# A state-space scan whose chunk states are stored adjacently, with carries in doubling steps, corrections tile by tile, and gating between its steps

## What is computed

```python
x_re = jnp.einsum('bngc,gpc->bngp', ug, bb_re)      # 64 groups, 16 channels, 64 states
x_im = jnp.einsum('bngc,gpc->bngp', ug, bb_im)
...
_, _, s_re, s_im = lax.associative_scan(combine, (l_re, l_im, x_re, x_im), axis=1)
y = (jnp.einsum('bngp,gcp->bngc', s_re, c_re)
     - jnp.einsum('bngp,gcp->bngc', s_im, c_im)).reshape(b_, n, D_MODEL)
y = jax.nn.gelu(y + d * uf)
out = (y @ w_glu_v) * jax.nn.sigmoid(y @ w_glu_g)
```

## Time and profile before

| | us |
|---|---|
| median of three runs | 2287.75 |
| the three runs | 2287.75, 2288.28, 2266.84 |
| the profiled execution: its time | 2266.89 |
| its span | 2264.6 |
| mean granted TensorE clock | 0.969 of full |
| PE busy | 2127.8 (94%) |
| DVE busy | 1087.0 (48%) |
| ACT busy | 745.5 (33%) |
| POOL busy | 157.2 (7%) |

### The profile page before, as it was taken

The page is one execution under the profiler, slowest core; times in us unless marked ns, Lnnn a source line. Parts: engine busy times, 40 slices in busy tenths (PEclk is TensorE's granted clock), DMA queues, the critical chain, the costliest instruction groups (busy, mean ns, idle before and its releaser), DMA issues.

```text
span 2264.6 us, 46747 instructions
## 1 busy us (share of the span) xinstructions
PE 2127.8 (94%) x19825; PEld 2020.4 (89%) x19825; DVE 1087.0 (48%) x1563; ACT 745.5 (33%) x1080; POOL 157.2 (7%) x250
## 2 busy tenths in 40 slices
PE   7999999974899999999999999988888799999998
PEld 6999999953899999999999999975656599999998
DVE  5453676697344445322654442234763234544422
ACT  4222222543343343222422222242543124434211
POOL 3002010140000000000000000000027100000000
PEclk9999999997999999999999999999999799999999
DMA  6232323100222333332333333221237322333332
GB/s 134 84 107 71 93 85 107 39 3 6 85 84 85 93 93 88 103 90 63 95 92 93 93 101 90 79 80 29 50 105 203 88 66 78 90 93 93 105 90 77
DMA packets 355924, 192.56 MB, mean 85 GB/s; under 512 B 33005, under 2 KB 350443, under 8 KB 355795
## 3 DMA queue, kind: packets, MB, share of 16 engines
q1 hardware_dynamic: 348736, 180.19, 27.8%
q0 software_dynamic: 5488, 9.03, 1.4%
q10 hardware_dynamic: 1570, 1.48, 0.3%
HBM read 184.23 MB, written 3.02 MB: 83 GB/s over the span
## 4 chain that ended last, share of the span: by engine, by line
PE 85%; DVE 7%; ACT 3%; SPq 2%; issue 2%; DMA 1%; DVEq 0%; ACTq 0%
PE ps L1724 75%; PE ps L1737 2%; DVE stmp L466 2%; PE ps L2132 1%; PE ps L2257 1%; DVE xs L470 1%; PE ps L2288 1%; SPq L440 1%; SPq L438 1%; DVE stmp L469 1%; PE ps L2019 1%; PE ps L1743 1%; DVE wl L1126 1%; PE ps L2235 1%; DMA xin<-x_prompt 0%
## 5 line engine op out<-in xcount | busy, mean ns | idle before, releaser
L1724 PE MATMUL ps<-xh,wh 128*128 128x260 f32 x3296 | 870.1, 285 | 30.8 <-DVE xl L1441 15.8
L1724 PE MATMUL ps<-xl,wh 128*128 128x260 f32 x3296 | 863.6, 284 | 0.0
L1724 PE MATMUL ps<-xh,wl 128*128 128x260 f32 x3296 | 667.4, 284 | 0.0
L1724 PEld LDWEIGHTS ps<-xh,wh 128*128 128x128 f32 x3296 | 626.9, 190 | 37.7 <-issue 30.6
L1724 PEld LDWEIGHTS ps<-xl,wh 128*128 128x128 f32 x3296 | 625.0, 190 | 0.0
L1724 PEld LDWEIGHTS ps<-xh,wl 128*128 128x128 f32 x3296 | 512.1, 190 | 0.0
L650 ACT ACTIVATE wh<-raw 128x1024 fp32r<-128x1024 f32 (+1 forms) x150 | 175.6, 1170 | 597.7 <-PE ps L1724 596.5
L1126 DVE TENSOR_TENSOR wl<-raw,wh 128x1024 fp32r<-128x1024 f32 (+1 forms) x150 | 206.1, 1374 | 238.9 <-ACT wh L650 238.8
L1724 PE MATMUL ps<-hh,wh 128*128 128x260 f32 x1056 | 277.7, 284 | 0.0
L1724 PE MATMUL ps<-hl,wh 128*128 128x260 f32 x1056 | 275.6, 282 | 0.0
L668 ACT ACTIVATE wh<-raw 128x1024 fp32r<-128x1024 f32 (+1 forms) x124 | 135.3, 1091 | 418.3 <-PE ps L1724 418.3
(11 more groups left out here) (403 smaller groups left out, 2200.3 us busy)
## 6 DMA issues: line engine op xcount, KB each, us to landing
raw<-ffn_w_gate SPq DMA_DIRECT2D x88, 512.0 KB, 3.8
raw<-ffn_w_up SPq DMA_DIRECT2D x88, 512.0 KB, 3.8
raw<-ffn_w_down SPq DMA_DIRECT2D x64, 704.0 KB, 4.5
cb<-cache_ckv SPq DMA_DIRECT2D x72, 128.0 KB, 2.8
cb<-cache_ckv POOLq DMA_DIRECT2D x56, 128.0 KB, 2.9
raw<-s_w_glu_v SPq DMA_DIRECT2D x8, 512.0 KB, 3.8
raw<-s_w_glu_g SPq DMA_DIRECT2D x8, 512.0 KB, 3.7
raw<-mla_w_o SPq DMA_DIRECT2D x8, 512.0 KB, 4.1
```

The lines of the kernel that those rows point to most:

```text
L1724: got = mm(ps[0:width, bank + half, 0:HALF], w[par_][:, k * width:k * width + width], src[:, k0 + k, half * HALF:half * HALF + HALF], star ...
```

## The change

1. `xs` becomes [128, re/im, 32 pairs, 8 (m), 9 (b)]: the blocks b of one m lie side by side, in rows nine apart. ACT's `chunk_inputs` writes it with two instructions for each of re and im. PE's `from_states` reads it with b outside and m inside, nine words apart.
2. The carries take three doubling steps (distance 1, 2, 4) with two more powers `mu2`, made by POOL; the corrections run tile by tile, 4 pairs and 7 x 7 numbers at once, and raise `s_sc` per tile.
3. During scan part 2, DVE runs a piece of the gating of tiles 0 to 3 after each step (`first_tiles`).
4. d u is added to the taps matrix (`s_kd`), so the gating reads PSUM and `ta` is not needed. `ct` copies for tiles 2 to 5 move from POOL to ACT, written out between ACT's other work. Bank 3 serves tiles 3 and 7.
5. `xh` and `xl` stay in position order; the addition to x turns the order back.
6. PE: taps and from_states 2 and 3 in turns, then taps 4 to 7, then from_states 4 to 7; the GLU waits for `s_q7` and for the tiles one by one.

```diff
-                u, xs, s0, sn, wba = take(
-                    a, ("u", [P, KD, TOK], F32), ("xs", [P, 2, NPAIR, NCH + 1], F32), ("s0", [P, 2, NPAIR, NB], F32),
+                u, xs, sn, wba = take(
+                    a, ("u", [P, KD, TOK], F32), ("xs", [P, 2, NPAIR, NBK, NB8 + 1], F32),
...
+            def block(m, b0, b1):
+                return xs[:, :, lo:hi, 0, b0 + 1:b1 + 1] if m == NBK - 1 else xs[:, :, lo:hi, m + 1, b0:b1]
...
             for m in range(1, NBK):
-                own(advance(blk[:, :, :, :, m], blk[:, :, :, :, m - 1], 0, nb))
-            for b in range(1, nb):
-                own(advance(blk[:, :, :, b:b + 1, NBK - 1], blk[:, :, :, b - 1:b, NBK - 1], NBK - 1, 1))
-            for m in range(NBK - 1):
-                got = advance(blk[:, :, :, 1:nb, m], blk[:, :, :, 0:nb - 1, NBK - 1], m, nb - 1)
+                advance(block(m, 0, NB8), block(m - 1, 0, NB8), mu[:, 0], NB8)
+                if beside is not None:
+                    beside(step)
+                step += 1
+            for s, coef in ((1, mu[:, NBK - 1]), (2, mu2[:, 0]), (4, mu2[:, 1])):
+                advance(block(NBK - 1, s, NB8), block(NBK - 1, 0, NB8 - s), coef, NB8 - s)
...
+            for n0 in range(lo, hi, QP):
...
+                        got = tt(both[i][r], mu[:, 0:NBK - 1, 2 * i + r, n0:n0 + QP].rearrange("p m n -> p n m").unsqueeze(3).to_broadcast([P, *size]),
+                                 xs[:, i, n0:n0 + QP, 0, 1:NB8].unsqueeze(2).to_broadcast([P, *size]), ALU.mult)
...
+                own(tt(tmp[:, 0, 0:2 * w], tmp[:, 0, 0:2 * w], tmp[:, 1, 0:2 * w], ALU.add))
+                for r in range(2):
+                    part = xs[:, r, n0:n0 + QP, 1:NBK, 1:NB8]
+                    got = tt(part, part, both[0][r], ALU.add)
+                got.then_inc(done, 1)
...
-                run(xs[:, :, QP * t:QP * t + QP, 1:NCH + 1], x_ps[:, :, :, 0:NCH], ACT.Copy)
+                for r in range(2):
+                    x_b = x_ps[:, r, :, 0:NCH].rearrange("p q (b m) -> p q m b", m=NBK)
+                    run(xs[:, r, QP * t:QP * t + QP, 1:NBK, 0:NB8], x_b[:, :, 0:NBK - 1, :], ACT.Copy)
+                    run(xs[:, r, QP * t:QP * t + QP, 0, 1:NB8 + 1], x_b[:, :, NBK - 1, :], ACT.Copy)
...
+                if t >= 2:
+                    act.wait_ge(xl_rdy, GEN["glu"] + t - 1)
+                run(tb[:, t % 2, 0:SEQ], ps[:, Y_BANK[t], :], ACT.Square, scale=math.sqrt(0.044715)).then_inc(s_y2, 1)
...
+            tt(ktc[:, :, 0, :], ktc[:, :, 0, :], dd, ALU.add).then_inc(s_kd, 1)
...
+            chunk_scan(own, tt, stmp, NPAIR // 2, NPAIR, s_sc, first_tiles)
+            argument(4)
+            for t in range(5, KD):
+                gated(t - 1)
+                argument(t)
+                lo_out(t - 1)
...
-                tt(x[:, d, :], x[:, d, :], tb[:, j, :], ALU.add).then_inc(x_upd, 1)
+                tt(x[:, d, SEQ:TOK], x[:, d, SEQ:TOK], tb[:, j, SEQ:TOK], ALU.add)
+                by_step = x[:, d, 0:SEQ].rearrange("p (c i) -> p i c", i=L)
+                tt(by_step, by_step, tb[:, j, 0:SEQ].rearrange("p (i c) -> p i c", i=L), ALU.add).then_inc(x_upd, 1)
...
-                pe.wait_ge(s_sc, 1 if t < KD // 2 else 2)
+                pe.wait_ge(s_sc, t + 1)
...
-                                             xs[:, r, QP * t + q, 0:NCH], start=False, stop=i == L - 1 and r == 1, skip_group_check=True)
+                                             xs[:, r, QP * t + q, :, 0:NB8].rearrange("p m b -> p b m"), start=False, stop=i == L - 1 and r == 1, skip_group_check=True)
...
-            for t in range(2, KD):
+            pool.wait_ge(s_ct, CT[5])
+            for t in range(6, KD):
                 out_matrices(t)
```

More of the change, by code:

```diff
@@ L469, in advance @@
                 own(tt(both[0], both[0], both[1], ALU.add))
[L470 removed]
+                own(tt(dst, dst, both[0], ALU.add))
+            step = 0
             for m in range(1, NBK):
[L473 to L481 removed]
+                advance(block(m, 0, NB8), block(m - 1, 0, NB8), mu[:, 0], NB8)
+                if beside is not None:
+                    beside(step)
+                step += 1
@@ L881, in _, with out_matrices @@
             tap_blocks(3)
+            def out_matrices(t):
+                act.wait_ge(s_ct, CT_0 if t == 2 else CT[t - 1])
+                act.wait_ge(s_yp, t - 1)
+                for h in range(2):
+                    rows = slice(NS * h, NS * h + NS)
+                    for r in range(2):
+                        last = run(ct[rows, t % 2, :, r, :].rearrange("p j (q h c) -> p j q h c", q=QP, h=2)[:, :, :, h, :],
+                                   ctc[rows, r, QP * t:QP * t + QP, :, :].rearrange("p q j c -> p j q c"), ACT.Copy)
+                last.then_inc(s_ct, 1)
@@ L882, in _ @@
+            squared(0)
+            sigmoid(0)
+            hi_out(0)
+            out_matrices(3)
+            squared(1)
+            sigmoid(1)
+            hi_out(1)
+            tap_blocks(4)
+            squared(2)
+            sigmoid(2)
+            hi_out(2)
+            out_matrices(4)
+            squared(3)
+            sigmoid(3)
+            hi_out(3)
             act.wait_ge(s_fp, 1)
-            run(s0[:, :, :, :].rearrange("p r n b -> p (r n b)"), ps[:, 6, :], ACT.Copy).then_inc(s_fe, 1)
@@ L884, in _ @@
-            tap_blocks(4)
+            run(sn[:, :, :, :].rearrange("p r n b -> p (r n b)"), ps[:, 6, :], ACT.Copy).then_inc(s_fe, 1)
             tap_blocks(5)
+            out_matrices(5)
             tap_blocks(6)
+            tap_blocks(7)
             act.wait_ge(s_fe, 1)
@@ L1400, in _ @@
             dve.wait_ge(s_ctc, L)
-            dve.wait_ge(s_w, W_MU)
[L1402 to L1405, removed]
+            same = stmp[:, 0, 0:GC]
+            own(V.tensor_reduce(same, cst[:, C_ST:C_ST + NS].rearrange("p (k c) -> p c k", c=GC), AX.X, ALU.add))
+            dd = stmp[:, 1, 0:KD * GC].rearrange("p (t c) -> p t c", c=GC)
@@ L1442, in _ @@
+            chunk_scan(own, tt, stmp, NPAIR // 2, NPAIR, s_sc, first_tiles)
+            argument(4)
+            for t in range(5, KD):
+                gated(t - 1)
+                argument(t)
+                lo_out(t - 1)
+            dve.wait_ge(s_q6, 1)
+            tt(xl[:, :, SEQ:TOK], ysb, xh[:, :, SEQ:TOK], ALU.subtract).then_inc(s_q7, 1)
             gated(KD - 1)
@@ L2518, in _ @@
                 m = 2 * m
-                if m < NBK:
+                own(last)
+            for k in range(2):
+                src = mu2[:, 0] if k else mu[:, NBK - 1]
+                t0, t1 = (kfree[:, 256 * i:256 * i + 2 * NPAIR].rearrange("p (r n) -> p r n", r=2) for i in range(2))
+                T(t0, src[:, 0:1, :].to_broadcast([P, 2, NPAIR]), src[:, 0:2, :], ALU.mult)
+                own(T(t1, src[:, 1:2, :].to_broadcast([P, 2, NPAIR]), src[:, 2:4, :], ALU.mult))
+                own(T(mu2[:, k, 0:2, :], t0, t1, ALU.add))
+                G.tensor_scalar(mu2[:, k, 2, :], mu2[:, k, 1, :], -1.0, None, ALU.mult)
+                last = G.tensor_copy(mu2[:, k, 3, :], mu2[:, k, 0, :])
+                if k == 0:
                     own(last)
```

167 lines of the change are left out of this document (97 added, 70 removed).

## The result

The changed kernel takes 2255.87 us in the median of 20 runs (2242.34 to 2274.50), the kernel before 2286.72 in the median of 20 runs beside them (2266.80 to 2291.83). The ratio is 0.9892, with a 95% interval from 0.9869 to 0.9916: about one per cent faster. The forecast was 2266.7, within 2240 to 2279.

What follows compares the result with a forecast made beforehand. It took one chain, DVE alone then DVE and ACT in turns from 450.16 to 572.10 us, as the bound. Its terms put the GLU at 551.0, 21.1 sooner: 2287.75 - 21.1 = 2266.7 us, range 2240 to 2279.

Steps and rivals of the forecast that it cites:

- Chunk inputs: ACT's unpacking before the scan: four instructions for one, 0.5 us more a tile, mostly hidden; scan starts at 450.7.
- Part 1: First scan part on DVE: 27.0 us of own work plus 5 of surcharge beside POOL's copies, 32.0 us.
- Part 2: Second scan part on DVE with gating between steps: 482.7 to 520.7, with 0.7 a tile operation and 1.5 of late ACT answers.
- Adjacency: DVE's scan operations on xs in runs of 8 and 7: 1.1 ns a number, bounds 1.04 and 1.9.
- Taps 5: PE's start of taps 5 after ACT's taps block 5: 520.2, after some 9 us of idleness.
- A tile from states: PE's matmuls reading xs nine words apart: 2.5 us a tile, bounds 2.00 (no effect) and 4.0 (double).
- the ring: ACT and DVE alternating over the last tiles' output, remainder, square, sigmoid and product: 3.4 us a turn.
- Rival 2: PE pays for the stride of xs, 4 us a tile: GLU at 555, 17 gained, 2271; chance 0.12.
- GLU: In the GLU, x's big addition goes from 0.70 to about 1.3 us; priced at nothing, 0.6 with no cover.
- 0.37 + 3 x 0.47: DVE's scan step over 256 numbers in the new layout, summed to 1.75 us against 2.33 before.
- Rival 3: PE pays far more for the stride: slower from 7.8 us a tile, 18 slower at 10, 2306; chance 0.04.
- such a fall of the median: The measured median falling into the lower group of runs, as one of three did; adds about 0.15.

Runs made afterwards that it cites:

- the second profile: The changed kernel itself run once more with nothing altered, profiled at full clock in the chunk inputs: 2244.69 us.
- the run of the scan alone: The kernel before with only the new layout, doubling scan and tile-wise corrections, without interleaved gating or moved copies: 2251.43 us, ratio 0.9881.
- the two runs in turns: The changed kernel with taps and from_states alternating on PE and ACT's work earlier: states read in stored order 2255.45 us, with step 9 2239.28 us.
- the fill: Dense fp32 products that nobody reads, added before the chunk inputs: five on the changed kernel 2250.48 us, five on the kernel before 2281.36 us.

## Why the prediction was right, step by step

At the clock of the profile behind the prediction the sum held almost to the microsecond: the GLU at 550.52 against 551.0, 21.6 us gained against 21.1, 22.2 in time. The mechanism was right: the shorter scan alone gives 19 of the 22. That the sum came so near is in part luck, for two of its errors cancel. Step by step, in the second profile:

- **Chunk inputs.** Scan from 449.82, predicted 450.7. The four copies for one cost nothing that shows.
- **Part 1** 32.25 us, predicted 32.0 (27.0 of work and 5 of surcharge). It was right as a sum: the work is about 26 and POOL takes 6. Single steps go from 1.72 to 3.0 us beside POOL's copies (453.25, 461.40), and the last doubling step takes 3.9 beside POOL's arithmetic for the sample, where the same step takes 1.2 in part 2. In the run of the scan alone, with POOL's copies beside part 2 as well, part 2 took 33.1 us.
- **Part 2** 35.8 us, predicted 38.0. The gating operations cost 0.61 each and not 0.7, and the waits for ACT came to 1.8 us, priced at 1.5.
- **Adjacency.** 256 numbers in runs of eight take 0.42 to 0.43 us, the same as over adjacent scratch, and 0.46 from start to start, so about 1.04 ns a number beside the 0.2 us, the near end of my bounds. Every other row begins at an odd word. The Trainium skill (Vector Engine (DVE) Microarchitecture Reference, Measured stream behaviour on trn2) gives 1.30 ns for pairs that begin so; with runs of eight no such loss is to be seen.
- **Taps 5** at 517.49, predicted 520.2, after 7.34 us of idleness; and 14.0 us for the three, as predicted.
- **A tile from states** is the term that was mis-sized: 2.5 us predicted, 4.0 measured. The steps of 16 bytes and more double the pass. And even without it the term had been 3.9, for the four tiles stand back to back. That could be read before. The first profile of the kernel before has tiles back to back, the second of these 3.9 us behind the first:

```profile
500.28 2.00 PE L2047 MATMUL ps<-xs,ct 128*32 128x64 f32 x127 [0.38 <-issue]
504.18 2.00 PE L2047 MATMUL ps<-xs,ct 128*32 128x64 f32 x128 [1.90 <-issue]
```

I took the 2.00 of a tile between taps and left the 1.90 of "issue" beside it unread. The loss was hidden by the 2.8 us won in front (the last four tiles start at 531.49, not 534.3) and by the ring: I had the last tiles 3.4 us apart through ACT and DVE, and they came 3.8 to 3.9 apart through PE. Rival 2, which had the right price for the tile, put the GLU at 555 for the same reason: it kept the late start of taps 5.
- **GLU.** The big addition to x takes 1.20 us in place of 0.70, ACT's square waits 2.7 us for it instead of 2.1, and PE is busy all of 560 to 580 us. Priced at nothing, rightly.
- **Slips in the working.** 0.37 + 3 x 0.47 is 1.78 and not 1.75, 0.2 us a part; measured 1.72. Rival 3 has the kernel even at 7.8 us a tile and 18 slower at 10: with the four tiles that it names that is 9, and 18 would take all eight.

**The number.** 2266.7 was the median of three runs less 21.1, and the measured one is 10.8 below it. What I had not seen is that the gain depends on the clock. At half clock in the chunk inputs the kernel before loses 12.7 us of the GLU's start and the changed one 21.1 (550.52 to 571.60). The first profile of the changed kernel shows where:

```profile
503.24 0.22 DVE L1504 TENSOR_TENSOR rbc<-rbc,ps 128x64 f32<-128x64 f32 x1 [7.32 <-PE ps L2148]
```

Part 2 of the scan begins at 492.62 there, 10.6 us later than at full clock. After its first step DVE has a piece of the sample's gating to do, and waits 7.32 us for the sample's product on PE, which stands behind the late chunk inputs and taps; the scan ends at 538.20, 20.4 later, and ACT's taps block 5, the taps and the tiles are as late as that. In the kernel before, the sample's gating stands behind the scan and does not wait for PE. So the interleaving ties the scan to PE, and the prediction had no term for it, since its profile had the full clock.

The gain is 22 in one pair of profiles and 13 in the other, yet the median fell by 31, because more runs of the changed kernel (10 of 20) than of the kernel before (3 of 20) fell in their lowest group. The part of the 31 beyond 22 is the mixture and nothing that the prediction worked out; it gave such a fall of the median 0.15. Whether the change raises that chance or the sample was kind stays open: in the twelve later runs the changed kernel had four in its lowest group and a median of 2264.44, and the kernel before had medians of 2281.58, 2277.18 and 2278.16 in its later sets.

## What to carry to other kernels

When a stage is cut short on one engine, look up who paces the next one before counting the rest of the gain: here the scan alone gave 19 of 22 us, and some 16 more lay in PE's and ACT's order and in the stride of PE's operand. An operation that is moved in between the steps of a long chain brings its own waits into the chain: ask what it waits for when the engine that feeds it is late. Price a block of small matmuls by the distance from one to the next where they stand back to back, "issue" included, and keep the moving operands of such small fp32 matmuls at a step of at most two numbers: scatter on the PSUM side instead, which cost nothing here. When the times of a kernel lie in groups, profile until each group has a profile, and compare like with like; a median over groups says more of their mixture than of the change.

## What the runs showed of the hardware that was not expected

- 128 matmuls of 64 fp32 numbers take 2.0 to 2.2 us with steps of 1 and 2 in the moving operand, and 3.6 to 4.2 us with steps of 4, 8, 9 and 16; PSUM written with a step of 8 costs nothing (2.00).
- PE's instructions came in packets of about 16 KB, one for 128 small matmuls with their weight loads. No two packets started less than 3.2 us apart in fourteen traces; tiles of 2.00 us back to back came every 3.9 us, with halts of 1.6 to 1.9 us. That the packets set this pace is likely, not shown.
- The granted clock fell to half at 434 us in six of ten profiles without dense products in front, some 2 us into a stage of matmuls of 32 rows that kept PE busy throughout, and stayed there for 61 us. In four profiles with two or five dense products just ahead of it, it never fell in this stage, and 18 of 18 runs of the changed kernels with them have a mean of 0.972 or more, where 21 of 44 did without them in the changed kernel and the two runs in turns. Only six of the 18 ran beside runs without a fill (11 of 24 of these at 0.972 or more). In the kernel before the mean doesn't tell, for with the fill it is 0.959 to 0.968. That the fill is the cause is likely by these counts; how it works is not shown, and the fill also starts the stage 1 us or more later, which was not tried by itself.
